# One score matrix for both key groups, and two retention heads per step

## What is computed

```python
# compressed keys: 8 query heads in 2 groups, 15 keys (n_c) for each group
s_c = jnp.einsum('bqghd,bngd->bghqn', qb, k_cmp) + head_bias(dist_c)
p_c = _masked_softmax(s_c, dist_c >= 0)
o_c = jnp.einsum('bghqn,bngd->bqghd', p_c, v_cmp)
...
# retention, 4 heads of 64: scores within a chunk, times a decay
inner = jnp.einsum('bnchd,bnehd->bnhce', qc, kc).astype(jnp.float32) * decay
o_inner = jnp.einsum('bnhce,bnehv->bnchv', inner, vc)
```

## Time and profile before

| | us |
|---|---|
| median of 3 runs | 1244.37 (1244.36 to 1247.01) |
| the profiled execution | 1244.34 |
| its span in the trace | 1242.5 |
| TensorE busy in the span | 1189.4 |
| VectorE busy | 852.7 |
| ScalarE busy | 549.0 |

### The profile page before, as it was taken

The page is one execution under the profiler, slowest core; times in us unless marked ns, Lnnn a source line. Parts: engine busy times, 40 slices in busy tenths (PEclk is TensorE's granted clock), DMA queues, the critical chain, the costliest instruction groups (busy, mean ns, idle before and its releaser), DMA issues.

```text
span 1242.5 us, 17275 instructions
## 1 busy us (share of the span) xinstructions
PE 1189.4 (96%) x6920; PEld 1018.9 (82%) x6920; DVE 852.7 (69%) x1327; ACT 549.0 (44%) x687; POOL 35.3 (3%) x43
## 2 busy tenths in 40 slices
PE   7999999999999798999999999998798999999996
PEld 5788788887997687787999888997687788999885
DVE  4466466556698898787677554698888777777442
ACT  5554565544435444443534333434453543543431
POOL 0222000000000000000000000000000000000000
PEclk9999999999999999999999999999899999999999
DMA  8456655347545224354455555454232454455540
GB/s 301 148 195 228 211 153 166 105 151 257 170 142 198 104 103 136 125 180 169 170 180 194 201 194 203 155 190 143 100 129 102 148 191 170 170 176 197 202 153 34
DMA packets 39467, 206.54 MB, mean 166 GB/s; under 512 B 4003, under 2 KB 13731, under 8 KB 16307
## 3 DMA queue, kind: packets, MB, share of 16 engines
q1 hardware_dynamic: 39052, 205.22, 48.2%
q10 hardware_dynamic: 336, 0.22, 0.1%
HBM read 204.23 MB, written 1.20 MB: 165 GB/s over the span
## 4 chain that ended last, share of the span: by engine, by line
PE 76%; DVE 15%; DVEq 4%; issue 2%; ACT 2%; DMA 0%; POOL 0%; POOLq 0%; ACTq 0%
PE panel L883 17%; PE panel L885 16%; PE panel L884 16%; PE panel L906 6%; PE panel L905 6%; PE panel L904 6%; DVE area L2010 4%; DVE ring_parts L576 4%; PE tile L933 4%; DVEq L2011 2%; PE heads_out L1092 1%; ACT ring_parts L551 1%; DVEq L2079 1%; PE tile L991 1%; PE panel L923 1%
## 5 line engine op out<-in xcount | busy, mean ns | idle before, releaser
L576 DVE TENSOR_TENSOR ring_parts<-ring,ring_parts 128x2048 fp32r<-128x2048 f32 (+1 forms) x185 | 415.4, 2257 | 159.0 <-ACT ring_parts L551 155.1
L551 ACT ACTIVATE ring_parts<-ring 128x2048 fp32r<-128x2048 f32 (+1 forms) x185 | 348.6, 1888 | 261.1 <-PE panel L885 205.0
L883 PE MATMUL panel<-ring_parts,hT_high 128*128 128x512 f32 (+2 forms) x688 | 282.9, 411 | 14.7 <-DVE ring_parts L576 11.6
L885 PE MATMUL panel<-ring_parts,hT_low 128*128 128x512 f32 (+2 forms) x688 | 267.4, 389 | 0.0
L884 PE MATMUL panel<-ring_parts,hT_high 128*128 128x512 f32 (+2 forms) x688 | 266.7, 388 | 0.0
L904 PE MATMUL panel<-hT_high,ring_parts 128*128 128x256 f32 x704 | 199.4, 283 | 0.0
L906 PE MATMUL panel<-hT_high,ring_parts 128*128 128x256 f32 x704 | 199.2, 283 | 0.0
L905 PE MATMUL panel<-hT_low,ring_parts 128*128 128x256 f32 x704 | 199.2, 283 | 0.0
L883 PEld LDWEIGHTS panel<-ring_parts,hT_high 128*128 128x128 f32 x688 | 131.2, 191 | 54.3 <-issue 27.6
L885 PEld LDWEIGHTS panel<-ring_parts,hT_low 128*128 128x128 f32 x688 | 131.0, 190 | 27.4
L883 PE MATMUL panel<-ring_parts,area_parts 128*128 128x512 f32 x384 | 150.6, 392 | 0.0
(11 more groups left out here) (227 smaller groups left out, 1100.0 us busy)
## 6 DMA issues: line engine op xcount, KB each, us to landing
ring<-in_w_layers_dram SPq DMA_DIRECT2D x140, 1024.0 KB, 4.9
ring<-in_w_first_dram SPq DMA_DIRECT2D x40, 1024.0 KB, 5.0
area<-bias_rows SPq DMA_DIRECT2D x16, 160.0 KB, 3.1
ring<-in_w_layers_dram SPq DMA_DIRECT2D x4, 560.0 KB, 4.1
area<-bias_rows SPq DMA_DIRECT2D x16, 96.0 KB, 2.9
area<-bias_rows SPq DMA_DIRECT2D x1, 1536.0 KB, 8.8
area<-in_gains_dram SPq DMA_DIRECT2D x3, 512.0 KB, 5.7
x<-in_x_dram SPq DMA_DIRECT2D x2, 512.0 KB, 4.7
```

Source lines behind the costliest of these rows:

```text
L551: act.activation(ring_lo[:, SLOTS + hi, 0:w], ring[:, slot, 0:w], ACT.Copy).then_inc(high_ready, 1)
L576: g.tensor_tensor(ring_lo[:, slot, 0:w], ring[:, slot, 0:w], ring_lo[:, SLOTS + hi, 0:w], ALU.subtract).then_inc(low_ready, 1)
L883: pe.matmul(ps[:, b, 0:width], high, hi[:, k, :], start=first, stop=False)
L885: mm = pe.matmul(ps[:, b, 0:width], low, hi[:, k, :], start=False, stop=last)
```

## The change

The compressed keys of the two groups are laid on the diagonal of one matrix of 128 rows and 30 columns: group 0 on rows 0 to 63 of columns 0 to 14, group 1 on rows 64 to 127 of columns 15 to 29, zero elsewhere. A new memset of VectorE clears the matrix in each layer, after the low part of `k4/1` (ahead of L2030), and ScalarE fills the two blocks with two copies instead of one. One matmul with all 128 rows then gives two heads, one of each group: eight matmuls of 30 columns in place of sixteen of 15, in one tile in place of two. VectorE reads them in two additions of 120 columns in place of four of 60.

The retention scores are made for two heads in one step, R0 with R1 after step 7 of `mg0` and R2 with R3 after step 2 of `mg1`. The two heads alternate: both matmuls of 256 columns, then both of 128, each on its own half of the array's rows and into its own tile. VectorE's `decayed` is called for both heads in the same step.

```diff
-    ("mg0", 7): ["R0"], ("mg1", 0): ["R1"], ("mg1", 2): ["R2"], ("mg1", 5): ["R3"], ("mg4", 2): ["oR"], ("mg5", 1): ["cv"],
+    ("mg0", 7): ["R0"], ("mg1", 2): ["R2"], ("mg4", 2): ["oR"], ("mg5", 1): ["cv"],
...
-            elif e == "cmpS":
-                out += ["cmpS0", "cmpS1"]
+            elif e in ("R0", "R2"):
+                out += [e, f"R{int(e[1]) + 1}"]
...
-                    for g in range(2):
-                        ps, done = tile_after(part, f"cmpS{g}", ["cmp2"] if g == 0 else [])
-                        for b in range(NB):
-                            for i in range(4):
-                                r, c = head_rows(4 * g + i)
-                                s = (b * 4 + i) * N_CMP
-                                mm = pe.matmul(ps[:, s:s + N_CMP], qT[r, c, b * P:(b + 1) * P],
-                                               two("kcmpT")[r, g * N_CMP:(g + 1) * N_CMP], start=True, stop=True)
-                        mm.then_inc(done, 1)
+                    ps, done = tile_after(part, "cmpS", ["cmp2"])
+                    for b in range(NB):
+                        for c in range(4):
+                            s = (b * 4 + c) * 2 * N_CMP
+                            mm = pe.matmul(ps[:, s:s + 2 * N_CMP], qT[:, c, b * P:(b + 1) * P], two("kcmpT")[:, 0:2 * N_CMP],
+                                           start=True, stop=True)
+                    mm.then_inc(done, 1)
...
-                    ps, done = tile_after(part, f"R{h}", transposed("rot") if h == 0 else [])
-                    r = slice(HD * (h % 2), HD * (h % 2) + HD)
-                    pe.matmul(ps[:, 0:TOKENS], rT[r, 2 + h // 2, 0:P], rT[r, h // 2, :], start=True, stop=True)
-                    pe.matmul(ps[:, TOKENS:TOKENS + P], rT[r, 2 + h // 2, P:TOKENS], rT[r, h // 2, P:TOKENS],
-                              start=True, stop=True).then_inc(done, 1)
+                    heads = (h, h + 1)
+                    outs = [tile_after(part, f"R{i}", transposed("rot") if i == 0 else []) for i in heads]
+                    rows = [slice(HD * (i % 2), HD * (i % 2) + HD) for i in heads]
+                    for (ps, _), r in zip(outs, rows):
+                        pe.matmul(ps[:, 0:TOKENS], rT[r, 2 + h // 2, 0:P], rT[r, h // 2, :], start=True, stop=True)
+                    for (ps, done), r in zip(outs, rows):
+                        pe.matmul(ps[:, TOKENS:TOKENS + P], rT[r, 2 + h // 2, P:TOKENS], rT[r, h // 2, P:TOKENS],
+                                  start=True, stop=True).then_inc(done, 1)
...
-                        act.activation(two("kcmpT")[:, 0:30], ps[:, 0:30], ACT.Copy, scale=0.5)
+                        for g in range(2):
+                            r, n = slice(HD * g, HD * g + HD), slice(g * N_CMP, (g + 1) * N_CMP)
+                            act.activation(two("kcmpT")[r, n], ps[r, n], ACT.Copy, scale=0.5)
...
                 lows_to(part, "k4/1")
+                v.memset(two("kcmpT"), 0.0)
                 blk = two("blk").rearrange("p (i j n) -> p i j n", i=2, j=16)
...
-                    for g in range(2):
-                        ps = tile_of(v, part, f"cmpS{g}")
-                        for b in range(NB):
-                            s = 31 + P * (1 - b)
-                            src = ps[:, b * 4 * N_CMP:(b + 1) * 4 * N_CMP].rearrange("p (h n) -> p h n", h=4)
-                            hg = slice(4 * g, 4 * g + 4)
-                            e = v.tensor_tensor(Lc[:, b, hg], src, En[:, hg, backwards(s, N_CMP, CMP_STRIDE)], ALU.add)
-                        e.then_inc(tile_sem(part, f"cmpS{g}"), 1)
+                    ps = tile_of(v, part, "cmpS")
+                    scores = ps[:, 0:16 * N_CMP].rearrange("p (b c g n) -> p b g c n", b=2, c=4, g=2)
+                    for b in range(NB):
+                        s = 31 + P * (1 - b)
+                        e = v.tensor_tensor(Lc[:, b].rearrange("p (g c) n -> p g c n", g=2), scores[:, b],
+                                            En[:, :, backwards(s, N_CMP, CMP_STRIDE)].rearrange("p (g c) n -> p g c n", g=2), ALU.add)
+                    e.then_inc(tile_sem(part, "cmpS"), 1)
...
                     elif e[0] == "R":
                         decayed(int(e[1]))
+                        decayed(int(e[1]) + 1)
```

## The result

| | before | after |
|---|---|---|
| median of 5 runs, us | 1244.37 (1244.22 to 1247.01) | 1237.37 (1237.04 to 1240.60) |
| span of the profiled execution | 1242.5 | 1235.5 |
| TensorE busy | 1189.4 | 1183.5 |
| VectorE busy | 852.7 | 852.2 |

The change is worth 7.0 us, a ratio of 0.9945 with a 95% interval of 0.9929 to 0.9962.

What follows compares the result with a forecast made beforehand. VectorE was taken to bound the changed stretch, 450.81 to 509.48 us. Idle time and additions less memset gave 1.24 and 1.20 us in the layers, together 2.4, hence 1241.9; range 1240.8 to 1243.1, widened to 1240.0 to 1244.4 for 8 in 10.

Steps and rivals of the forecast that it cites:

- its idle time of 1.04 and 1.10 us: VectorE's wait for the first window pair's scores, layers 0 and 1: forecast to vanish, bringing the taps sooner by that much.
- R1's move: On VectorE, R1's decay of 0.54 us goes from behind the first window pair to ahead of `compressed_out`: net 0.
- the next pair: Scores of the following window pair: readable at 464.4, VectorE there at about 466.0, so no wait, 1.6 us in hand.
- the wait of TensorE at the transpose of the second window head: TensorE waits 1.2 us from about 458.7 until VectorE has read R2's tile: new, but free.
- TensorE's saving: Compressed scores save 1.6 us and paired retention heads 1.8: up to 3.4 a layer, none of it counted by itself.
- Rival A: TensorE was the bound after all and its whole saving of 6.8 us comes through: 1237.7 us; chance 0.09.
- The additions: On VectorE's compressed scores, two of 120 columns replace four of 60: gain 0.3 us in layer 0, 0.2 in layer 1.
- The memset: On VectorE ahead of L2038, clearing the key matrix: charged 0.1 us in each layer.
- The new waits: TensorE waits for VectorE to read R0 (0.2 us, first window pair) and R2 (1.2 us, second window head's transpose).
- The range: Own range 1241.3 to 1242.6 us; with 0.5 us by which fast runs may differ, 1240.8 to 1243.1.
- rival C: Longer TensorE waits let the clock fall behind 509; each layer loses 1.9 us and gains 1.2: 1245.7; chance 0.10.
- The price of the narrow matmuls: Sixteen compressed-score matmuls on TensorE cost 3.25 us, 0.20 each; the eight remaining take 1.6 and save 1.6.

Runs made afterwards that it cites:

- the filled pair: Kernels before and after, each with unread wide matmuls in two TensorE waits per layer (first transpose, start of `mg0`): medians 1242.39 and 1235.17 us.
- the kernel with the scores cut in two: Kernel before with the eight compressed-score matmuls of group 0 moved one `mg0` step earlier: median 1242.94 us; with both waits filled 1240.65.
- the three new traces: Kernel before, unchanged, traced three more times: spans 1244.7, 1245.6 and 1242.1 us.
- the filled kernel before: Kernel before with seven unread matmuls of 512 columns ahead of each layer's first transpose: median 1244.55 us, ratio 1.0005.

## Why the prediction was wrong

**What held.** VectorE sets the pace behind the pair: its idle time of 1.04 and 1.10 us closed, R1's move cost nothing, the next pair was not waited for, and the wait of TensorE at the transpose of the second window head was free. TensorE's saving, 3.15 us in a layer by the rows after (3.25 - 1.76 for the scores, 4 x 0.84 - 2 x 0.85 for the retention), is not what arrived: 1.6 and 1.8 did. Both halves together bring hardly more than one. Rival A, at 1237.7, hit the number, but not by its mechanism.

**Terms that were mis-sized.** The additions gained 0.10 and 0.13 (0.86 to 0.76, 0.77 to 0.64), not 0.3 and 0.2: the PSUM row of rows 6 was too cheap a neighbour, two of 120 took nearer to the spread pattern's 0.35 each. The memset was charged with 0.1 and cost nothing; at 365.94 VectorE doesn't set the pace. The new waits measured 0.46 and 0.66, not 0.2 and 1.2. Two gaps in VectorE's order that I had not counted became shorter. Before, at the retention output of layer 0 and ahead of R2's decay in layer 1:

```profile
474.61 1.36 DVE L2178 TENSOR_SCALAR area<-panel,bna,stat 128x128 f32<-128x128 f32 x4 [0.44 <-issue]
...
921.27 0.42 DVE L2149 TENSOR_TENSOR area<-tile,decay 128x256 f32<-128x256 f32 x1 [0.57 <-issue]
```

After:

```profile
470.77 1.44 DVE L2181 TENSOR_SCALAR area<-panel,bna,stat 128x128 f32<-128x128 f32 x4
...
914.23 0.42 DVE L2152 TENSOR_TENSOR area<-tile,decay 128x256 f32<-128x256 f32 x1 [0.19 <-issue]
```

That is 0.4 in each layer that the sum lacked; what these gaps are was not looked into. The work is 3.4 us in place of the forecast 2.4, which alone would have given 1240.9, just inside the range. The range itself allowed 0.5 us for differences between runs, though the three runs shown ahead of it lay up to 2.65 us apart (1244.36 to 1247.01).

**The step that failed** is the clock. The sum was made against one trace, as if its half-rate stretches were part of the kernel, and rival C let the clock fall only where TensorE waits. But the removed work itself makes it fall: in the sixteen narrow matmuls and behind them three of four traces of the kernel before are at half rate for 3 to 7 us in one layer or both, worth 1.5 to 3.1 us each in B0 or B1, and neither trace of the changed kernel is at half rate there. Only the first trace, from which I costed, had none there; it had 3.1 us of half rate behind the first transposes instead, so that its time was near the median all the same; that was luck. The price of the narrow matmuls was read as 3.25 us, their own time, and lacked what they do to the wide ones behind them. In the filled pair, where the traces of both kernels are free of other half-rate stretches in A and at the start of `mg0`, the whole difference of the spans (1240.65 and 1233.98, 6.7 us) lies in B0 and B1. How it divides is an estimate: with 3.4 of work as without filling, 3.3 are half rate; with the prices of the unfilled traces, 1.5 us for the shorter stretch and 3.1 for the longer, 4.6 are half rate and 2.1 work. For the second speaks that filling alone shortened B1 of the kernel with the scores cut in two from 57.09 to 56.55, with no half rate there in either trace. For the medians of the unfilled kernels it is an estimate too: 7.0 less the 3.4 of work leaves 3.6, and the three new traces have 4.6, 4.7 and 3.1 us of it in B0 and B1.

Rival C's mechanism is in the trace after, but free of cost. Behind the wait of 1.89 us at 490.30, at whose place the first trace of the kernel before stayed at full rate (behind 1.90 us at 494.07), the clock fell for most of the next 5 us:

```profile
490.00:495.00 5.00, 4.70 (x19) 3.13 (x20) 4.50 (x14) 2.90 (x5) 0.00 (x0) 0.66 0.45 184
```

B0 takes 63.83 us with it and 63.82 in the changed kernel with both waits filled, whose trace lacks it; and from 505.7 to 507.3, the place that rival C feared, the clock was 1.00. The rule of the Trainium skill (page "TensorE: Matmul & The Clock Gate", section "Why this matters for your kernels") that idle gaps between bursts bring TensorE back to half rate is borne out by these 1.89 us, and by the 2.01 us in A in one of four traces of the kernel before, though the page speaks of longer gaps; a wait of 1.70 us that leaves the clock up does not contradict it. But in the scores and behind them the clock also fell with no wait of TensorE in the 9 us ahead, in each of the ten cases counted above, and on that the change turned. The same page, section "Part 1: The HAM clock gate (the "warmup" mystery)", says that the count of slow matmuls at a kernel's start changes from run to run because the hardware's watching runs free of the kernel. The page says it of the start only; the four traces of one kernel, with half rate at other places in each, fit it.

**What stays open.** Which property of the narrow matmuls matters (columns, rows, or the time they fill) is not settled: the clock fell once behind eight of 15 columns with half the rows, behind eight of 30 with all rows in no trace. The six products with the values, of 64 columns, stand ahead of the scores in every one of these kernels, and no run took them away. The lowest runs of the unfilled kernels (1241.14 and 1236.35) differ by 4.8 us, more than the 3.4 of work; no trace of such a run of the kernel before was taken. Nor was one of the changed kernel's slower executions (1239.68 and 1240.60 of the five). Between A and B, behind the wait of 3.35 us, the four traces of the kernel before take 48.7 to 51.1 us in both layers together and the two of the changed one 49.0 and 48.7; whether the change has a part in that is not shown. And the 1.1 us at the start are not the change's: the first trace of the kernel before was the longest there, the three new ones are up to 1.7 us shorter, and the two of the changed kernel lie among them.

## What to carry to other kernels

A run of narrow matmuls costs its own time and may cost the clock of what follows, so price it from several traces of the same kernel, not from one, and look at the granted clock behind it even where TensorE never waits. Putting two halves of the array side by side, by a diagonal operand or by the order alone, shortens such a run. Where a wait ahead of TensorE-bound work lets the clock fall, wide matmuls that nobody reads can keep it up: with both waits filled 1237.37 became 1235.17 here, while the first wait alone gained nothing (1238.23).

## What the runs showed of the hardware

The granted clock fell to its lower level, 0.50, behind stretches in which TensorE was busy without a gap (889.80 to 893.20 in the filled kernel before), in or just behind sixteen matmuls of 15 columns with 64 rows, one half of the array after the other, or sixteen of 30 columns with 128 rows: in 10 of 16 layers of eight traces. After seven of 512 and eight of 30 it stayed at 1.00 in both layers of one trace, and after eight of 30 alone or sixteen of 15 on alternate halves in all 14 layers of seven. Executions of one program, the kernel before, lay between 1241.14 and 1249.72 us, and its four traces differ by where half-rate stretches fell. Sixteen matmuls of 15 columns on alternate halves of the array took 1.89 us, against 3.25 one half after the other.
